# Result rows numbered in the order of the units, loaded and summed in six groups while the last units run

## What is computed

```python
    scores = jax.nn.sigmoid((hf @ router_w).astype(jnp.float32))
    sel = scores + router_bias.astype(jnp.float32)
...
    _, idx = lax.top_k(jnp.where(emask, sel, -jnp.inf), TOP_K)
    wts = jnp.take_along_axis(scores, idx, axis=-1)
    wts = wts / jnp.sum(wts, axis=-1, keepdims=True) * ROUTED_SCALE
    routed = routed_experts(hf, idx, wts.astype(h.dtype), w_gate, w_up, w_down)
    shared = swiglu(hf, sw_gate, sw_up, sw_down)
...
        x = x + g2 * moe_ffn(h, router_w[l], router_bias[l], exp_w_gate[l], exp_w_up[l], exp_w_down[l],
                             sh_w_gate[l], sh_w_up[l], sh_w_down[l])
    return rms_norm(x, final_g)
```

## Time and profile before

| what | value |
|---|---|
| median of three runs | 2722.73 us (2720.15 to 2723.53) |
| the profiled execution | 2720.02 us |
| its span, first to last instruction | 2718.3 us |
| mean granted TensorE clock | 0.973 of full speed |
| busy: PE, VectorE, ScalarE, GpSimd | 2561.3, 1069.0, 667.0, 598.6 us |
| the units (first gate/up to last result piece) | 2090.8 to 2665.9 us |

### The profile page before, as it was taken

One profiled execution on the slowest core, in us unless ns is written; L12 is line 12 of the kernel. 1 busy time (PEld: TensorE's weight loads), 2 busy tenths in 40 slices (PEclk: granted clock), 3 DMA queues, 4 the chain that ended last, 5 costly groups with the idle time before them and its releaser, 6 DMA issues. The chain is left out here.

```text
span 2718.3 us, 30798 instructions
## 1 busy us (share of the span) xinstructions
PE 2561.3 (94%) x10853; PEld 1552.2 (57%) x10853; DVE 1069.0 (39%) x2302; ACT 667.0 (25%) x1318; POOL 598.6 (22%) x539
## 2 busy tenths in 40 slices
PE   8998999999999999999999999999999999999992
PEld 7546888445666488874445447656755434443440
DVE  1125888103323366650033335656533323322215
ACT  2223444202333222110035532122122111111111
POOL 3017887200000145421121001101110111111110
PEclk9999999999999999999999999999989999999996
DMA  4234565542111232323232120100034899999985
GB/s 134 78 93 139 167 173 160 124 89 63 51 55 55 77 94 77 93 77 82 74 83 74 34 51 11 26 31 16 24 152 165 352 421 413 402 385 399 401 335 225
DMA packets 290662, 404.56 MB, mean 149 GB/s; under 512 B 14419, under 2 KB 253737, under 8 KB 264433
## 3 DMA queue, kind: packets, MB, share of 16 engines
q1 hardware_dynamic: 273808, 366.24, 39.1%
q0 software_dynamic: 15632, 34.44, 3.9%
q10 hardware_dynamic: 1104, 2.31, 0.2%
HBM read 396.20 MB, written 27.71 MB: 156 GB/s over the span
## 5 line engine op out<-in xcount | busy, mean ns | idle before, releaser
L916 PE MATMUL bank<-bring 128*128 128x512 f32 x704 | 303.2, 592 | 0.0
L1649 PE MATMUL bank<-bring 128*64 128x512 f32 (+1 forms) x512 | 238.1, 620 | 17.4 <-issue 16.6
L916 PEld LDWEIGHTS bank<-bring 128*128 128x128 f32 x704 | 133.5, 190 | 166.1 <-issue 165.5
L977 PE MATMUL bank<-ysq 128*128 128x256 f32 x960 | 214.7, 380 | 0.0
L977 PEld LDWEIGHTS bank<-ysq 128*128 128x128 f32 x960 | 183.3, 191 | 25.2
L2179 DVE TENSOR_TENSOR xT<-bank,xT 128x512 f32<-128x512 f32 x32 | 22.1, 691 | 362.0 <-PE bank L916 361.9
L977 PE MATMUL bank<-hT,bring 128*128 128x256 f32 x640 | 144.7, 379 | 0.0
L681 POOL TENSOR_TENSOR ysq<-ysq 128x512 f32<-128x512 f32 x23 | 29.3, 1275 | 512.2 <-ACT ysq L1734 447.0
L1649 PEld LDWEIGHTS bank<-bring 128*64 128x64 f32 (+1 forms) x512 | 80.6, 163 | 104.6 <-issue 104.6
L690 POOL TENSOR_TENSOR two<-two 128x1024 f32<-128x1024 f32 (+2 forms) x72 | 121.3, 1685 | 72.7 <-ACT two L1754 51.8
L802 POOL TENSOR_TENSOR ffw<-two,maskT 128x512 f32<-128x512 f32 x40 | 52.2, 1315 | 383.8 <-DVE two L2568 316.5
(11 more groups left out here) (525 smaller groups left out, 4455.9 us busy)
## 6 DMA issues: line engine op xcount, KB each, us to landing
bring<-f_w_in SPq DMA_DIRECT2D x88, 512.0 KB, 5.2
bring<-exp_w_gate SPq DMA_DIRECT2D x32, 1024.0 KB
bring<-exp_w_up SPq DMA_DIRECT2D x32, 1024.0 KB
bring<-exp_w_down SPq DMA_DIRECT2D x32, 1024.0 KB, 21.4
two<-ada_w SPq DMA_DIRECT2D x24, 1024.0 KB, 5.3
bring<-f_w_down SPq DMA_DIRECT2D x16, 1408.0 KB, 7.1
two<-exp_w_gate SPq DMA_DIRECT2D x16, 1024.0 KB
two<-exp_w_up SPq DMA_DIRECT2D x16, 1024.0 KB
```

The lines of the kernel that those rows point to most:

```text
L916: mm = pe.matmul(ps[BANKS[stage][n % 4]][:], w[:, k, n % per * P:(n % per + 1) * P], rhs[:, k, :], start=(k == 0), stop=(k == kb - 1))
L977: mm = pe.matmul(ps[bank][:, 256 * half:256 * half + 256], weights[:, k, :], rhs[:, k, :], start=(k == 0), stop=(k == 3))
L1649: mm = pe.matmul(ps[3][m * h:m * h + m, :].rearrange("p (m n) -> p m n", m=2), hgT[par][:, k, m * h:m * h + m], w, start=(k == 0), stop=(k ...
```

## The change

Result rows are numbered in the order of the places, not of the experts. VectorE's running sum is made behind the permutation instead of ahead of it (TensorE now transposes and moves the mask `wtok`), so row j of a token is the j-th of its six places. Row 0 can then come from place 58 at the latest, row 1 from 59, and so on up to row 5 from place 63. The scores, which `wj` is picked from, have to be moved by the same permutation: four transposes behind unit 0 on TensorE, a copy on ScalarE, four products behind unit 1, and `wj` is picked in the iterations of units 3 to 5.

The 12 loads are cut by row number: group j is row j of all tokens, in two loads of 1 MB (two token tiles each, 4 KB a token). Groups 0 and 1 go out when unit 40's rows are stored and the buffers are free, group 2 behind unit 41, groups 3 and 4 behind unit 42, group 5 behind unit 43 and the overflow branch. From unit 41 on (`SOON`), a unit's down product, result pieces and scatter stand in its own iteration. VectorE sums group 0 behind the results of unit 42, group 1 between the activation and the results of unit 43, groups 2 to 4 behind those, and group 5 behind the overflow branch. The sum is held in the tile of group 0. The four norms stand together at the end.

```diff
+SOON = len(UNITS) - 3
...
-        ytok = [w.rearrange("p (j d) -> p j d", j=6) for w in exw]
+        Y_AT = (((0, 0), (0, 2)), ((0, 4), (1, 0)), ((1, 2), (2, 0)), ((2, 2), (1, 4)), ((2, 4), (3, 0)), ((3, 2), (3, 4)))
+        ypair = lambda j, n: exw[Y_AT[j][n][0]][:, Y_AT[j][n][1] * D:(Y_AT[j][n][1] + 2) * D].rearrange("p (t d) -> p t d", t=2)
+        yrows = lambda j, t: ypair(j, t // 2)[:, t % 2, :]
+        Y_SEMS = (("ring0_loaded", "ring1_loaded"), ("up0_loaded", "up1_loaded"), ("expgu0_loaded", "expdn0_loaded"),
+                  ("expgu1_loaded", "expdn1_loaded"), ("expgu2_loaded", "expdn2_loaded"), ("expgu3_loaded", "expdn3_loaded"))
...
-            sp.wait_ge(s("exp_down"), 2 * len(UNITS))
+            def results_in(j, n, sem_name):
+                rows = y_dram.rearrange("(t p j) d -> p t j d", p=P, j=8)[:, 2 * n:2 * n + 2, j, :]
+                sp.dma_start(ypair(j, n), rows).then_inc(s(sem_name), 16)
+
+            last = len(UNITS) - 1
+            sp.wait_ge(s("exp_gu"), last - 1)
+            sp.wait_ge(s("y0_stored"), 16 * (last // 2))
+            sp.wait_ge(s("y1_stored"), 16 * (last // 2 - 1))
+            results_in(0, 0, Y_SEMS[0][0])
+            results_in(0, 1, Y_SEMS[0][1])
+            sp.wait_ge(s("exp_down"), 2 * last - 2)
+            results_in(1, 0, Y_SEMS[1][0])
+            sp.wait_ge(s("exp_gu"), last)
+            results_in(1, 1, Y_SEMS[1][1])
+            sp.wait_ge(s("y1_stored"), 16 * (last // 2))
+            results_in(2, 0, Y_SEMS[2][0])
+            results_in(2, 1, Y_SEMS[2][1])
+            sp.wait_ge(s("exp_down"), 2 * last)
+            sp.wait_ge(s("y0_stored"), 16 * (last // 2 + 1))
+            results_in(3, 0, Y_SEMS[3][0])
+            results_in(3, 1, Y_SEMS[3][1])
+            results_in(4, 0, Y_SEMS[4][0])
+            sp.wait_ge(s("exp_gu"), last + 1)
+            results_in(4, 1, Y_SEMS[4][1])
...
+            sp.wait_ge(s("exp_down"), 2 * len(UNITS))
             overflow_rounds(sp, overflow_loads, end=overflow_moved)
 
-            for par in range(2):
-                sp.wait_ge(s(f"y{par}_stored"), 8 * len(UNITS))
-            sp.wait_ge(s("exp_down"), 2 * len(UNITS))
-            for t in range(TT):
-                for j in range(0, 6, 2):
-                    sp.dma_start(ytok[t][:, j:j + 2, :], y_dram.rearrange("(t p j) d -> p t j d", p=P, j=8)[:, t, j:j + 2, :])\
-                        .then_inc(s(sems_of(t)[j // 4]), 16)
+            sp.wait_ge(s("y1_stored"), 16 * (last // 2 + 1))
+            results_in(5, 0, Y_SEMS[5][0])
+            results_in(5, 1, Y_SEMS[5][1])
...
             for u in range(len(UNITS)):
                 if u + 2 < len(UNITS):
                     gather(u + 2)
-                if u:
+                if 0 < u <= SOON:
                     results_out(u - 1)
-            results_out(len(UNITS) - 1)
+                if u >= SOON:
+                    results_out(u)
...
-                tr = pe.transpose(ps[0][0:EXPERTS, t * P:(t + 1) * P], nth_sel[:, t, :], ident[:])
+                tr = pe.transpose(ps[0][0:EXPERTS, t * P:(t + 1) * P], wtok[:, t, :], ident[:])
...
-                if u:
+                if 0 < u <= SOON:
                     finish(u - 1)
                 wait(pe, s("exp_actT"), u)
                 for k in range(2):
                     pe.wait_ge(s("exp_act"), 2 * u + k + 1)
                     turned = turn_act_half(par, k)
                 turned.then_inc(s("exp_turned"), 1)
-            finish(len(UNITS) - 1)
+                if u >= SOON:
+                    finish(u)
+                if u == 0:
+                    for t in range(TT):
+                        tr = pe.transpose(ps[7][0:EXPERTS, t * P:(t + 1) * P], sco[:, t, :], ident[:])
+                    tr.then_inc(s("rt_prod"), 1)
+                if u == 1:
+                    pe.wait_ge(s("front_act"), 6)
+                    for t in range(TT):
+                        mm = pe.matmul(ps[7][:, t * EXPERTS:(t + 1) * EXPERTS], nthT[:, t * P:(t + 1) * P], place_at,
+                                       start=True, stop=True)
+                    mm.then_inc(s("rt_prod"), 1)
...
+                if u == 0:
+                    act_e.wait_ge(s("rt_prod"), 8)
+                    nc.scalar.copy(nthT, ps[7][0:EXPERTS, :]).then_inc(s("front_act"), 1)
...
-            order(nc.vector.tensor_scalar(row_parts[:, :, :, 0], moved, row_base, None, ALU.add))
+            dve.wait_ge(s("rt_step"), 5)
+            order(nc.vector.tensor_tensor_scan(flat(nth_sel), cmask[:, 0:256], flat(pos), 0.0, ALU.mult, ALU.add))
+            nc.vector.tensor_tensor(nth_sel, nth_sel, pos, ALU.mult).then_inc(s("rt_step"), 1)
+            dve.wait_ge(s("rt_step"), 6)
+            order(nc.vector.tensor_scalar(row_parts[:, :, :, 0], nth_sel, row_base, None, ALU.add))
             dve.wait_ge(s("rt_prod"), 6)
...
             def weights_of(js):
 
+                dve.wait_ge(s("rt_prod"), 9)
                 for j in js:
-                    order(nc.vector.scalar_tensor_tensor(out=pick, in0=nth_sel, scalar=float(j + 1), in1=sco,
+                    order(nc.vector.scalar_tensor_tensor(out=pick, in0=nth_sel, scalar=float(j + 1), in1=placed_sco,
                                                          op0=ALU.is_equal, op1=ALU.mult))
...
+            def weighted(j, t):
+                return nc.vector.scalar_tensor_tensor(out=yrows(0, t), in0=yrows(j, t), scalar=wj[:, t, j:j + 1],
+                                                      in1=yrows(0, t) if j else res[:, t, :], op0=ALU.mult, op1=ALU.add)
+
+            def combine(j):
+                for t in range(TT):
+                    if t % 2 == 0:
+                        dve.wait_ge(s(Y_SEMS[j][t // 2]), y_loaded(j, t // 2))
+                    wait(dve, s("y_summed"), TT * (j - 1) + t + 1)
+                    weighted(j, t).then_inc(s("y_summed"), 1)
 
             for u in range(len(UNITS)):
                 par = u % 2
@@ -2806,11 +2869,18 @@
                     act_half(par, k).then_inc(s("exp_act"), 1)
                 if u + 2 < len(UNITS):
                     slot_tokens(u + 2)
-                if u:
+                if u == len(UNITS) - 1:
+                    combine(1)
+                if 0 < u <= SOON:
                     results(u - 1)
-                if u < 3:
-                    weights_of((2 * u, 2 * u + 1))
-            results(len(UNITS) - 1)
+                if 3 <= u < 6:
+                    weights_of((2 * u - 6, 2 * u - 5))
+                if u >= SOON:
+                    results(u)
+                if u == len(UNITS) - 2:
+                    combine(0)
+            for j in range(2, 5):
+                combine(j)
...
-            overflow_rounds(dve, overflow_expert, beyond)
+            def combined_again():
+                dve.wait_ge(s("ov_loaded"), 48 * ROUNDS * EXPERTS + 160)
+                for j in range(5):
+                    for t in range(TT):
+                        left(weighted(j, t))
+
+            overflow_rounds(dve, overflow_expert, beyond, end=combined_again)
+            combine(5)
 
...
-            for t in range(TT):
-                for j in range(6):
-                    if j == 0:
-                        dve.wait_ge(s(f"expgu{t}_loaded"), 32 * (EXPERTS // 4 + 1))
-                    elif j == 4:
-                        dve.wait_ge(s(f"expdn{t}_loaded"), 16 * (EXPERTS // 4 + 1))
-                    wait(dve, s("y_summed"), 6 * t + j if j else 0)
-                    nc.vector.scalar_tensor_tensor(out=res[:, t, :], in0=ytok[t][:, j, :], scalar=wj[:, t, j:j + 1], in1=res[:, t, :],
-                                                   op0=ALU.mult, op1=ALU.add).then_inc(s("y_summed"), 1)
-                if t:
-                    last_norm(t - 1)
+            for t in range(TT - 1):
+                last_norm(t)
             last_norm(TT - 1)
 
 

```

30 lines of the change are left out of this document (17 added, 13 removed).

## The result

The changed kernel takes 2700.86 us (median of four runs, 2700.77 to 2703.79) against 2723.13 of the kernel before: ratio 0.9921, 95% interval 0.9904 to 0.9938. Timed twice more for the experiments, it gave 0.9939 (0.9925 to 0.9952) and 0.9944 (0.9931 to 0.9958), so the mean of the three, 0.9935 or some 18 us, is the better value of the gain. The profiled execution is 2700.77 us, its span 2699.0 (2718.3 before), the mean granted clock 0.976.

A forecast was written before the change was run, and what follows sets the result against it. Bound: VectorE's sums and late loads in a 52.45 us tail after the last arithmetic. 22.3 - 1.7 - 1.0 - 0.5 = 19.1 us off 2720.02 gives 2700.9; half of 2.7 added: 2702 us, range 2696 to 2711.

The forecast's parts named there:

- The tail after T: Behind the last unit's arithmetic: 16 sums, flag skip, four scalings and last store take 30.1 us against 52.45, 22.3 gained.
- The branch: Skip over the overflow code, now between groups 4 and 5 on VectorE: 0.5 us taken, 0 to 4.4 possible.
- T: End of the last unit's result pieces, 2665.85 before: 2667.5 from the end of the units, before anything earlier moves it.
- the routing: Extra transposes and small products on PE in units 0 and 1: delay of 0 to 1.7 us, 1.0 taken.
- the end of the units: Units 41 to 43 with down products moved forward and group sums on VectorE between them: T 1.7 us later.
- rival (a): End of the units: down weights land at 2650.5, PE idles 3 us, clock falls; 2707 to 2712 us, chance 0.17.
- FIFO order gives the weights the front: Argument against late down weights for unit 42, which were expected to land anywhere from 2646 to 2650.5.
- Group 1 ahead of the last pieces: Four sums (5.2 us) on VectorE between unit 43's activation and results: they, no longer TensorE, set T.
- The loads: Result-row loads for groups 2 to 5: slack 2 to 3 us, group 5 stalls VectorE 0 to 1.5, 0.5 taken.
- (c): Table loads: 4 KB reads of single rows halve the load rate or worse, so DMA bounds the end; chance 0.05.
- (d): VectorE stalls on each group in turn, 10 us or less gained: 2713 to 2725 us, chance 0.06.
- signs that I had set for "wrong": VectorE load wait over 2 us; PE idle ahead of down(42), clock 0.5; late unit 4; flag gap; table loads under 400 GB/s.

The follow-up runs named there:

- after_again: The changed kernel itself, unaltered, timed and traced a second time: 2705.07 us (2702.01 to 2705.83).
- after_third: The changed kernel itself, unaltered, timed and traced a third time: 2705.51 us (2700.77 to 2708.90).
- group1_behind: The changed kernel with group 1's four sums behind the last unit's result pieces instead of ahead of them: 2707.27 us, ratio 0.9951.
- unit_order_alone: The kernel before with only the order of units 41 to 43 changed; numbering, loads and sums as before: 2724.69 us, ratio 1.0015.
- down_by_act: The changed kernel with the down weights of places 62 and 63 issued from ScalarE's queue instead of SP's: 2703.55 us, ratio 0.9929.

## Why the prediction was right

**The tail after T** was the large term and held: 30.1 us and 0.5 of stall were forecast, 29.05 measured, 27.8 and 28.2 in the two later traces. The difference to the first is the sums at 1.20 to 1.25 us instead of 1.30 (each waits only for the one four back) and the branch, less 0.36 of stall. The four scalings take 5.7 and the last store 3.1, as forecast, and ScalarE's fourth root is ready 0.8 us ahead of VectorE.

**The branch** cost nothing in place of 0.5: it ran under a sum. Its VectorE rows are 567 ns for the flag (560 before) and 68 for the branch (68 before). The 3 us by the rule of the Trainium skill ("Runtime: NRT & Kernel Launch", instruction fetch mechanics) were not met on VectorE; PE's branch took 5.86 us, behind its last product.

**T** was the step that failed in size. I had it 1.0 us later by the routing and 1.7 by the end of the units, at 2668.5; it is 2669.95, 2675.4 and 2670.8. Since unit 0 starts at another time in each trace, it has to be taken apart. The shifts against the kernel before are:

| trace | start of unit 0 | from there to gate/up of unit 41 | from there to T |
|---|---|---|---|
| forecast | 0 | 1.0 | 1.7 |
| changed kernel, first | 0.7 | 4.8 | -1.4 |
| `after_again` | 4.0 | 1.4 | 4.1 |
| `after_third` | 0.2 | 1.3 | 3.4 |

The routing's 1.0 is right (0.95 at unit 2). In the first trace, the T near the forecast is luck: two terms missed by 3.8 and 3.1 us in opposite directions. In the two later traces the end of the units costs two times the forecast and more, and that is what rival (a) described and I gave 0.17: the down weights do not land by 2650.5 but at 2651 to 2655, TensorE mostly waits 3.5 to 4 us for them, and the clock falls behind that, for 1.7 to 2.6 us more. "FIFO order gives the weights the front" was the wrong argument: the weights stood ahead of the loads of the rows, but behind 5 MB of other weights, and landed 13.4 to 16.6 us after their issue. The page of the kernel before could have warned me, with a median of 21.4 us to landing for the down weights that go into `bring`. That (a) did not bring its 2707 to 2712 is a wrong sum: its own terms (T at 2671, a tail of 30.1, 2 us for group 5, 1.7 from span to time) give 2705 to 2706, which is near the 2705.1 and 2705.5 of the two later timings.

**Group 1 ahead of the last pieces** was taken as what sets T. It does, but by 0.7 us only: down(43) ends at 2668.52 and the pieces follow at 2668.67, both in one go, where `group1_behind` has T 0.7 us sooner after the start of down(43).

**The loads** held VectorE up for 0.84 us ahead of T (group 0) and 0.86 behind it (group 4, where 0.5 within 0 to 1.5 was forecast for group 5). The last scatter (8.20, forecast 3.3 to 9.3) and group 5's load (6.46, forecast 7.4) balance VectorE to within 0.1 us. Reads of single rows at 387 GB/s left (c) without ground; (d), half the cover gone, was not seen. VectorE hardly waits for loads: 1.7 us in the first trace, nothing over 0.3 us in the two later ones.

Two of the signs that I had set for "wrong" did appear: loads of the table under 400 GB/s (387, which cost nothing that can be told), and TensorE idle ahead of down(42) with the clock at its lower level behind it, in both later traces.

In all, 2702 was forecast; 2700.9, 2705.1 and 2705.5 were measured, with the kernel before 1 to 3 us lower in the later comparisons. That the time lies so near is in part luck: the tail came 1.5 to 2.8 us shorter than its 30.6, and T 1.4, 6.9 and 2.3 us later than its 2668.5, of which 4.0 in the second trace stand ahead of the units.

## What to carry to other kernels

Work behind the last arithmetic can be moved under it where the DMA share there is near zero. As that share fills, a small transfer in the chain takes longer: here the last scatter took 8.2 us and not 3.3, and the sum should use the longer time from the start. Moving a consumer of weights forward gained nothing by itself here (`unit_order_alone`), because the weights landed 13 to 30 us after their issue, and it cost the engine's clock; look at when a transfer lands, not at its place in the queue. Where a chain has two bounds of one length, take something from both or leave it. And before a T from one trace is compared with a T from another, subtract a point that stands ahead of the change: here that point moved by up to 5 us.

## What the runs showed of the hardware

- The last scatter of 128 rows took 3.19 to 3.47 us with no loads beside it, 4.78 with group 4's 2 MB held back, and 8.19 to 8.83 with all loads issued.
- In `down_by_act`, a transfer of 1 MB issued 4 us after two others that landed within 12 us landed 30.5 us after its issue; one issued 12 us later from ScalarE's queue overtook it (10.4).
- VectorE's 128x1024 sums took 1.20 to 1.25 us each when none needed the one just before, and 1.32 when each did (six in 7.95); beside a GpSimd product of 128x1024 (3.31 us) two of them took 4.36.
- Behind TensorE's waits of over 4 us in the units (4.07 to 5.98) its granted clock was at the lower level each time. Behind shorter ones it was or was not: it fell after 2.23 us at 2588.45 in `after_again`, and not after 3.67 at 2611.62 in `unit_order_alone` or 3.18 at 2585.21 in `after_third`. With the wait ahead of down(42) filled by products that nothing reads it stayed at 1.00.
- A product of 128x512 with 128 columns of weights is counted as two matmuls, one starting every 0.44 us (12 in 5.3 us).
